# A two-bits-a-round search, pool sums on GpSimd, and the sample's attention placed within the attention units

## What is computed

```python
def layer(x, pos, attn_fn, pool_prev, conv_prev, p):
    h = rms_norm(x, p['g_pre_mix'])
    q, k, v, qi, ki, wi, xp = project(h, p['w_in'], pos)       # q, k, qi, ki rotated (rope)
    a = attn_fn(q, k, v, qi, ki, wi)
    m = pool_mixer(concat([pool_prev, xp], axis=1), T, p['w_pool'], p['pool_scale'])
    mix = concatenate([a, m], axis=-1) @ p['w_out']
    ...                                                        # residual, then the conv FFN

def indexer_scores(qi, wi, ki, q_pos, k_pos):
    dots = einsum('bqhd,bld->bqhl', qi, ki) * (IDX_DIM ** -0.5)
    s = einsum('bqhl,bqh->bql', relu(dots), wi) * (N_IDX_HEADS ** -0.5)
    return where(k_pos <= q_pos, s, -inf)

# prompt: for each block of 128 queries, the 128 best keys; sample: the 256 best of 2049
_, sel = lax.top_k(sc, topk)
p = softmax(where(sel <= q_pos, (q . k[sel]) * HEAD_DIM ** -0.5, -inf)); o = p . v[sel]

def pool_mixer(x_ext, n_out, w_pool, pool_scale):              # windows 2, 4, 8, 16
    diff = wsum / count - xg[:, R - n_out:]
    return einsum('btgc,gcd->btgd', diff, w_pool) * pool_scale
```

## Time and profile before

| | us |
|---|---|
| three runs | 1645.15, 1647.72, 1647.85 (median 1647.72) |
| the profiled execution | 1663.7 |
| span of its trace (first to last instruction) | 1661.9 |
| PE busy, PEld busy | 1499.6 (90%), 1288.6 (78%) |
| DVE busy, ACT busy, POOL busy | 810.7 (49%), 433.2 (26%), 144.3 (9%) |
| mean granted TensorE clock | 0.893 |

### The profile page before, as it was taken

How to read it: one execution, slowest core, us unless ns; L and a number is a source line. 1 busy time by engine, 2 the same in 40 slices (tenths; PEclk the granted TensorE clock), 3 DMA queues, 4 the chain that set the end, 5 groups by cost and what they waited for, 6 DMA issues and landing times. The chain is left out here.

```text
span 1661.9 us, 25466 instructions
## 1 busy us (share of the span) xinstructions
PE 1499.6 (90%) x9736; PEld 1288.6 (78%) x9736; DVE 810.7 (49%) x1716; ACT 433.2 (26%) x753; POOL 144.3 (9%) x160
## 2 busy tenths in 40 slices
PE   4999867899799999999998987699988999999995
PEld 3765744579699999999957556445878999999995
DVE  1137776242665555722142587742346565655221
ACT  3112023333422222522131120233333222224220
POOL 1000301200300000000040022040011000000002
PEclk8999965579899999999979999556789999999997
DMA  8870110102122222222259301010021222222221
GB/s 327 158 112 1 32 60 16 37 1 77 51 94 96 88 88 89 95 79 97 93 209 141 75 25 42 26 51 1 26 77 64 88 88 95 94 76 105 77 102 52
DMA packets 46317, 133.18 MB, mean 80 GB/s; under 512 B 6319, under 2 KB 25615, under 8 KB 38911
## 3 DMA queue, kind: packets, MB, share of 16 engines
q1 hardware_dynamic: 43423, 119.52, 24.9%
q0 software_dynamic: 2816, 12.62, 2.2%
HBM read 119.93 MB, written 12.82 MB: 80 GB/s over the span
## 5 line engine op out<-in xcount | busy, mean ns | idle before, releaser
L746 PE MATMUL ps<-moR_r,W_r 128*128 128x260 f32 x1408 | 286.1, 285 | 0.0
L746 PEld LDWEIGHTS ps<-moR_r,W_r 128*128 128x128 f32 x1408 | 219.1, 190 | 0.0
L746 PE MATMUL ps<-hT_r,QZC_r 128*128 128x260 f32 x896 | 185.1, 289 | 0.0
L746 PE MATMUL ps<-moR_r,QZC_r 128*128 128x260 f32 x704 | 146.7, 290 | 13.1 <-DVE hT_r L1756 12.8
L746 PEld LDWEIGHTS ps<-hT_r,QZC_r 128*128 128x128 f32 x896 | 143.0, 195 | 0.0
L746 PE MATMUL ps<-moR_r,SQ_r 128*128 128x260 f32 x704 | 142.1, 283 | 0.0
L746 PE MATMUL ps<-hT_r,SQ_r 128*128 128x260 f32 x704 | 140.5, 281 | 0.0
L733 PE MATMUL ps<-hT,W 128*128 128x260 f32 x576 | 139.0, 395 | 0.5 <-issue 0.5
L746 PEld LDWEIGHTS ps<-moR_r,QZC_r 128*128 128x128 f32 x704 | 110.8, 192 | 16.7 <-issue 8.5
L733 PEld LDWEIGHTS ps<-hT,W 128*128 128x128 f32 x576 | 109.9, 195 | 17.4 <-issue 1.1
L746 PEld LDWEIGHTS ps<-moR_r,SQ_r 128*128 128x128 f32 x704 | 108.6, 189 | 0.1
(11 more groups left out here) (304 smaller groups left out, 2791.0 us busy)
## 6 DMA issues: line engine op xcount, KB each, us to landing
W<-in_w_gates SPq DMA_DIRECT2D x44, 512.0 KB, 3.3
W<-in_w_vals SPq DMA_DIRECT2D x44, 512.0 KB, 3.3
W<-in_w_downs SPq DMA_DIRECT2D x16, 1408.0 KB, 6.0
W<-in_w_pairs SPq DMA_DIRECT2D x12, 1024.0 KB, 7.8
pages_by_slot<-moR SPq DMA_DIRECT2D x8, 1024.0 KB, 5.1
yR<-pages_by_slot SPq DMA_DIRECT2D x16, 512.0 KB, 19.5
W<-in_w_outs SPq DMA_DIRECT2D x8, 1024.0 KB, 4.8
W<-in_w_kv SPq DMA_DIRECT2D x2, 1312.0 KB, 10.5
```

The lines of the kernel that those rows point to most:

```text
L746: last = mm(ps[:, 2 * (g % 2) + f, 0:HT], w(k), x(k)[:, f * HT:(f + 1) * HT], start=(k == 0 and n == 0), stop=(k == nk - 1 and n == 2))
```

## The change

What is computed stays the same function of the inputs. What changes is this.

- The search tries **three candidates a round** and fixes two bits (`bit_pair`): 17 counts in place of 32. A round has three count operations of 128 x 129 in place of one, and two small operations in place of one ahead of the next candidates. PE sums three columns at a time.
- Rounds still run from d = 11 on. Beside the dots, a round is followed by one rank step in place of two; beside the query tiles by two in place of one. Pending counts are popped after **every fourth k** of a query tile in place of every second, and **pick_a, pick_b, pick_c** are popped there too; after the last round DVE does four rank steps and the last rotation. Units 0 to 3 have no rank steps now; 4 to 15 share the rest.
- The ends of the window sums go from DVE to **POOL** (`pooled`: five operations a window, after the last `cos_part` and before the list's DMA).
- The **pool tiles** go to unit 14 of PE's and ACT's order, as four matmuls of 512 columns and four of 8. SP's `load(9)` waits for these.
- The heads of a block are taken in the order 0, 4, 1, 5, ..., and the scores of the first block wait for the rotations of their own tile (PE has still waited for the last partner to be read).
- The sample's work moves: pick_d's operations to DVE units 0 to 3, its list to PE unit 6, pick_e from unit 14 to 9, keys turned at 21 to 24, scores at 26 and 28, softmax at 30 to 32, and the turn and the values of the sample to PE units 33 and 34, ahead of the last unit's values. ACT's `upper_out(0)` and DVE's `lower_mixed(0..3)` and `lower_out(0)` go from behind the units into them.
- Several tiles change their place in SBUF so that these lifetimes don't overlap.

The diff, cut to its core (ts, tt, stt are tensor_scalar, tensor_tensor and scalar_tensor_tensor on DVE):

```diff
-BITS = 31
+COUNTS = 2 + PAIRS
 SCORED = 10
-ROPES = {21: (4,), 25: (5,), 29: (6,), 31: (7,)}
-POOLED = {26: (0,), 27: (1,), 28: (2,), 30: (3,)}
-DVE_STEPS = 231
+ROPES = {16: (4,), 18: (5,), 19: (6,)}
+HEADS = (0, 4, 1, 5, 2, 6, 3, 7)
+DVE_STEPS = 211
 SPLITS = 2 * NF + 2 * KD
 
...
-                wait_alone(sp, *tile_done(l, WO_T))
+                wait_alone(sp, *pms_mm(l, 1))
                 load(9)
...
+            def pooled(l, g):
+
+                w = WINDOWS[g]
+                res = (LA[:, 0], LB[:, 0], LA[:, 2], LB[:, 2])[g]
+                edge = const("edge")[:, POOL_BUF * g:POOL_BUF * (g + 1)]
+                nc.gpsimd.tensor_tensor(res[:, 15:30], res[:, 15:30], edge, ALU.mult).then_inc(edge_done.sem, 1)
+                wait_alone(gp, *edge_done(l, 3 * g + 1))
+                nc.gpsimd.tensor_scalar(res[:, 15:527], res[:, 15:527], 1.0 / w, None, ALU.mult
+                                        ).then_inc(edge_done.sem, 1)
+                nc.gpsimd.tensor_scalar(DIFF[:, g, SEQ:TOK], XS[:, g, :], 1.0 / w - 1.0, None, ALU.mult
+                                        ).then_inc(edge_done.sem, 1)
+                wait_alone(gp, *edge_done(l, 3 * g + 3))
+                nc.gpsimd.tensor_tensor(DIFF[:, g, 0:SEQ], res[:, 15:527], XPb[:, g, 15:527], ALU.subtract
+                                        ).then_inc(diff_ready.sem, 1)
+                nc.gpsimd.tensor_tensor(DIFF[:, g, SEQ:TOK], DIFF[:, g, SEQ:TOK], prevs_all[:, l, 8 * g:8 * g + 8],
+                                        ALU.add).then_inc(diff_ready.sem, 1)
...
-                    if extras and k % 2:
+                    if extras and k % 4 == 3:
                         extras.pop(0)()
...
                             pe.wait_ge(*dot_relu(l, 24))
-                        mm(ps[:, count_bank(s), 300:301], const("same"), (cntB if s % 2 else cntA),
+                        n = 1 if s < 2 else 3
+                        mm(ps[:, count_bank(s), 300:300 + n], const("same"), tallies[s % 2][:, 0:n],
                            start=True, stop=True).then_inc(cnt_mm.sem, 1)
...
-                counts = [count(s) for s in range(1 + BITS)]
+                counts = [count(s) for s in range(COUNTS)] + [pick_a, pick_b, pick_c]
...
-                for step in counts:
-                    step()
-
                 pe.wait_ge(*rot_used(l, 8))
-                arrived(l, 7)
-                wp = wslot(7)[:, 0:512].rearrange("p (g d) -> p g d", g=4)
-                for g in range(4):
-                    pe.wait_ge(*evac(l, PM_T + g - 1))
-                    pe.wait_ge(*diff_ready(l, 2 * g + 2))
...
+                def pool_tiles():
+                    arrived(l, 7)
+                    wait_alone(pe, *list_ev(l, 1))
+                    pe.wait_ge(*o_ev(l, 1))
+                    wp = wslot(7)[:, 0:512].rearrange("p (g d) -> p g d", g=4)
+                    for g in range(4):
+                        pe.wait_ge(*evac(l, PM_T + g - 1))
+                        pe.wait_ge(*diff_ready(l, 2 * g + 2))
+                        mm(ps[:, 3 + 3 * (g % 2), :], wp[:, g, :], DIFF[:, g, 0:SEQ],
+                           start=True, stop=True).then_inc(tile_done.sem, 1)
+                    pe.wait_ge(*evac(l, PM_T + 3))
+                    for g in range(4):
+                        last = mm(ps[:, 3, NB * g:NB * (g + 1)], wp[:, g, :], DIFF[:, g, SEQ:TOK], start=True, stop=True)
+                    last.then_inc(pms_mm.sem, 1)
...
-                picks = {1: pick_a, 3: pick_b, 5: pick_c, 9: pick_d, 30: sample_scores, 32: scores_by_row}
-                picks.update({25 + q: (lambda q=q: keys_turned(q)) for q in range(4)})
+                picks = {6: pick_d, 14: pool_tiles, 26: sample_scores, 28: scores_by_row, 33: sample_probs_turned,
+                         34: sample_values}
+                picks.update({21 + q: (lambda q=q: keys_turned(q)) for q in range(4)})
 
                 def scores(i):
-                    t, h = divmod(i, N_HEADS)
+                    t, h = i // N_HEADS, HEADS[i % N_HEADS]
                     rows = slice(64 * (h // 4), 64 * (h // 4) + 64)
+                    if t == 0:
+                        pe.wait_ge(*rope_done(l, 5 + h % 4))
                     if i == 0:
-                        pe.wait_ge(*rope_done(l, 8))
-                        pe.wait_ge(*evac(l, WO_T))
+                        pe.wait_ge(*evac(l, PM_T))
...
                 def count(s):
-                    src, by = (S, 0.0) if s == 0 else (S2, cand)
-                    ts(J[:, :], src[:, :], by, None, ALU.is_ge, ALU.add, accum_out=(cntB if s % 2 else cntA)
-                       ).then_inc(cnt_ready.sem, 1)
+                    src, n = (S, 1) if s == 0 else (S2, 1 if s == 1 else 3)
+                    for i in range(n):
+                        last = ts(unread[i], src[:, :], cand(s, i).bitcast(F32) if s else 0.0, None, ALU.is_ge, ALU.add,
+                                  accum_out=tallies[s % 2][:, i:i + 1])
...
+                def bit_pair(s):
+
+                    n = 1 if s == 1 else 3
+                    b = 2 * (PAIRS + 1 - s)
                     dve.wait_ge(*cnt_mm(l, s + 1))
-                    then_wait(ts(candI[:, 1:2], counted(s), kth, float(1 << b), ALU.is_lt, ALU.mult))
-                    if b:
...
+                        then_wait(ts(passed_by, counted(s), kth, None, ALU.is_lt, ALU.add, accum_out=fails))
+                        then_wait(ts(fell, fails, float(1 << b), None, ALU.mult))
+                    top = cand(s, n - 1)
+                    if s + 1 < COUNTS:
+                        then_wait(stt(cands[(s + 1) % 2], bits[:, 3 * s - 3:3 * s], fell, top.broadcast_to([P, 3]),
                                       ALU.bitwise_or, ALU.bitwise_xor))
                         count(s + 1)
...
+                steps = [bits_start, bits_sign] + [lambda s=s: bit_pair(s) for s in range(1, COUNTS)] + [pick_b, pick_c]
...
-                        rank(2 if d >= 16 else 0)
+                        rank(1 if d >= 16 else 0)
                     else:
-                        rank(1)
+                        rank(2)
                     for j in ROPES.get(n, ()):
                         rope(j)
-                    for g in POOLED.get(n, ()):
-                        pooled(g)
-
-
-                def pick_a():
+                rank(4)
+                rope(7)
...
-                picks = {0: pick_a, 2: pick_b, 4: pick_c, 6: pick_d, 14: pick_e}
+                picks = {0: slots, 1: hot_high, 2: hot_low, 3: hot_rows, 9: pick_e, 30: sample_max, 32: sample_probs}
...
-                    if i < 2 * N_HEADS:
+                    if 4 <= i < 2 * N_HEADS:
                         rank(-(-len(ranks) // (2 * N_HEADS - i)))
...
+                    if i in (18, 20, 22, 24):
+                        lower_mixed(range(i // 2 - 9, i // 2 - 8))
+                    elif i == 28:
+                        lower_out(0)
```

More of the change, by code:

```diff
@@ L118, in constants @@
     c.view(np.int32)[:, lo:hi] = 0
-    for b in range(31):
-        c.view(np.int32)[:, lo + b] = 1 << b
+    for r in range(PAIRS):
+        for i in range(3):
+            c.view(np.int32)[:, lo + 3 * r + i] = (i + 1) << 2 * (PAIRS - 1 - r)
+    c.view(np.int32)[:, lo + 3 * PAIRS] = 1 << 2 * PAIRS
     return c
@@ L308, in build @@
         snew = sb("snew", [8, 1])
-        cols = sb("cols", [P, 16])
+        cols = sb("cols", [P, 20])
         sgn, kth, cntA, cntB, offs, need = (cols[:, i:i + 1] for i in range(6))
+        fails, passed_by = cols[:, 9:10], cols[:, 16:19]
+        tallies = [cols[:, a:a + 3] for a in (10, 13)]
+        unread = [yR[:, 3072 + 129 * i:3201 + 129 * i] for i in range(3)]
         snegc = cols[0:64, 6:7]
-        candI = sb("candI", [P, 2], I32)
+        candI = sb("candI", [P, 8], I32)
         IDX = sb("IDX", [P, NB, 2], I32)
@@ L852, in go, with pick_a, pick_b, pick_c @@
                             pe.wait_ge(*dot_relu(l, 24))
-                        mm(ps[:, count_bank(s), 300:301], const("same"), (cntB if s % 2 else cntA),
+                        n = 1 if s < 2 else 3
+                        mm(ps[:, count_bank(s), 300:300 + n], const("same"), tallies[s % 2][:, 0:n],
                            start=True, stop=True).then_inc(cnt_mm.sem, 1)
                     return go
-                counts = [count(s) for s in range(1 + BITS)]
+                def pick_a():
+                    wait_alone(pe, *pick_ready(l, 2))
+                    mm(ps[:, 4, 304:305], const("same"), cntA, start=True, stop=True).then_inc(pick_mm.sem, 1)
+                    mm(ps[:, 4, 305:306], const("below"), cntB, start=True, stop=True).then_inc(pick_mm.sem, 1)
+                def pick_b():
+                    wait_alone(pe, *pick_ready(l, 3))
+                    mm(ps[:, 4, 306:307], const("below"), cntA, start=True, stop=True).then_inc(pick_mm.sem, 1)
+                    mm(ps[0:64, 4, 307:308], const("newto"), J[:, 128:129], start=True, stop=True
```

(7 more changed lines are left out.)

289 lines of the change are left out of this document (150 added, 139 removed).

## The result

The changed kernel took **1588.49 us** (median of 4 runs, 1585.85 to 1601.40) against 1647.78 before (4 runs): ratio 0.966, interval 0.961 to 0.971. The profiled execution took 1585.85 us (span 1584.1, mean granted clock 0.932, before 0.893); the page has PE busy 1435.0 us, where it was 1499.6, though PE does nearly the same work.

What follows compares the result with a forecast made beforehand. The prediction took DVE and PE as nearly full beside the dots, PE to bound the query tiles, round trips the first scores, DVE units 0 to 15; terms summed to −12.6 us a layer, giving 1623 us, range 1603 to 1647.

Steps and rivals of the forecast that it cites:

- A, the dots: Search rounds beside the dots: longer rounds with three counts on DVE, +3.6 us a layer (bounds +2.3 and +5.0).
- B and C: Query tiles, PE-bound with fewer pops, −4.9 us a layer; then to first scores, a shorter chain of round trips, −13.1.
- D, units 0 to 15: DVE-bound units: more rank steps, the pool tiles and POOL holds outweigh removed picks, +6.4 us a layer.
- The hold by POOL: Units 0 to 3: POOL's moved sums hold DVE operations for 2.5 us a layer, a quarter of 10.4.
- E: Unit 16 to the output projection: fewer waits at the end and behind the gather, −4.6 us a layer (bounds −8, +5).
- rival 3: Fast stretch at 328.4 to 341.0 us loses its clock, costing 12.6 a layer: about 1647 us, chance 0.13.
- the waits that go: Before the output projection: sample's softmax and values chain moves beside units 30 to 32, −3.0 us a layer.
- the loss behind "remote": Middle units: DVE stood still 8.57 us during the gathers, PE lost 4.21; half taken as gone, −2.1 a layer.
- 1 (slower by the gather): Units 11 to 17: the earlier gather holds DVE while it is the bound; about 1654 us, chance 0.10.
- 2 (time comes back in the units): Units 0 to 15: full DVE–POOL holds (+7.9 a layer) or costlier rank steps and pool tiles; about 1638 us, chance 0.17.
- 4: Whole layer: all unknowns fall well, with no POOL hold and the gather stall gone; −21.5 a layer, 1605 us, chance 0.10.
- signs named for "wrong": PE waiting at query-tile counts, one-hot operations above 3 us, DVE idle in units 11 to 17, clock fallen before output projection.

Runs made afterwards that it cites:

- a_twice: The changed kernel with each of a round's three counts made twice, the second result unread: 1622.02 us, one execution.
- b_dense16: The kernel before with four added matmuls of 512 columns at PE's unit 16, whose result nobody reads: 1623.46 us, ratio to before 0.987.
- b_again: The kernel before, unchanged, in another profiled execution: 1647.56 us.
- a_pool20: The changed kernel with the pool tiles as one block at unit 20 in place of 14, banks, copies and low parts moved to fit: 1610.13 us.
- a_spread: The changed kernel with the pool tiles one matmul a unit at units 12 to 15 in place of all in unit 14: 1595.80 us.

## Why the prediction was right and wrong

**A, the dots**: forecast +3.6, measured +2.7 (175.7 against 173.0). Right in kind: in a_twice a round grows by what its counts grow, so DVE bounds the rounds.

**B and C**: forecast −4.9 and −13.1. The tiles take 32.6 where they took 38.4 (−5.8), and from the last tile to the first scores 6.3 where it was 19.3 (−13.0). Right. Taking cover and chain apart by stage was enough here; none of the PE waits at pops that I named as a danger is longer than 0.49 us in the tiles. No experiment undid the search alone; these two rest on the stage lengths of the two traces.

**D, units 0 to 15**: forecast +6.4, measured +9.4 against the earlier trace rows's execution between first scores and unit 16, +8.6 between the masks of units 0 and 16. The hold by POOL was forecast at 2.5 and measured at 2.6, but that it met is luck: a quarter was a guess, made since most operations there have one input from SBUF, and 1.74 of the 2.6 fell on just such operations. The pool tiles were forecast at 3 and measured at 4.0; the rank steps were eleven more, not ten. The rule that the prediction took from the Trainium skill (SBUF — State Buffer, Who interferes with whom) fits the one-hot operation, which has two inputs from SBUF. For the scalings, which have one, the same section of the Trainium skill lets a `tensor_scalar` contend when it runs in a two-port mode; that they did, no row here shows. The page Perfetto Trace Analysis of the Trainium skill, that moving work to GpSimd might not help, did not decide anything: the price is these 2.6 us, and what DVE was spared is part of C.

**E is the step that failed**: −4.6 forecast, −28.2 measured from unit 16 to the output projection. Another 1.2 us came behind it: the output projection starts at 0.50 in both, and is back at 1.00 after 3.2 us in place of 6.0, so that its first 40 records end 1.2 us sooner. The sum priced units 16 to 31 at the durations of the earlier trace rows and of their trace, at half clock, and asked only which waits would go. It said nothing of why the clock was 0.58 in one stretch and 1.00 in another, and rival 3 knew the clock only as something to lose, at a place (328 to 341 us) chosen since it was fast. I had the pool tiles' matmuls at unit 14 as a cost on PE, 3 to 6.8 us; that they raise the clock for what follows is the whole surprise. In numbers, with the second execution of before as the measure: −11.6 in units 16 to 23, by the clock; −12.2 from unit 24, of which b_dense16 with the old order of the tail gets 6.4 (52.6 to 46.2) by the clock, so that 5.8 are left for the moved softmax and values. (In layer 2 these are −9.4, 3.6 and again 5.8.) The forecast of 3.0 for the waits that go was right there, and most of the rest is the values' own time, 7.00 before and 3.74 now, which is the clock once more.

**A second fault lay in the base.** Half of the loss behind "remote", −2.1 a layer, was booked as a gain; another execution does not have the loss. The 16 us between profile and median were in view and were only passed on to the sum; they should have made every single stall in that trace suspect. The hold explains about half of the 16: units 16 to 23 were 4.3 a layer longer with it. Against b_again the stages sum to −28.6 in layer 1 and −25.3 in layer 2, −54 of the −59 between the medians; the output projections give another 2, and the rest was not followed.

**The rivals.** 1 (slower by the gather): no DVE wait behind "remote" in any trace of the changed kernel. 2 (time comes back in the units): partly, 3.0 of the 7.9 that it named. 3 (a fast stretch lost): not seen. The clock falls behind the sample's scores for 12.7 us, but it did so before too (335.4 to 345.6 us in b_again), and the units ahead gained a fast stretch. 4 named −21.5 a layer as the best case; the measured −29 lies beyond even the lower ends of A to E together (−26.7), since no term let PE's own durations change. Two of the signs named for "wrong" came, a one-hot operation of above 3 us (3.15) and a granted clock that has fallen ahead of the output projection; neither is what failed.

## What to carry to other kernels

Read the granted clock of each stretch beside its busy time before pricing anything in it: a stretch at 0.50 with PE busy throughout is not bound by its work but by a clock that something ahead of it did not raise. A reorder that puts long matmuls right ahead of many short ones can be worth more than all the waits that it removes: b_dense16 gained 21 us by nothing else. Whether taking out short waits between matmuls does the same was not tried by itself. And take the base from an execution that is near the median; a stall seen once is checked in a second trace before it is booked.

## What the runs showed of the hardware

- PE busy without a gap does not by itself raise the clock: 29.3 us of the kernel before (b_again) and 16 us in a_pool20 passed at 0.50, with matmuls of 128 and 384 columns. The same units ran at 1.00 behind the pool tiles (17.7 us). So the same code ran through at either level.
- It rose within four matmuls of 512 columns (after, a_pool20, b_dense16), and with such matmuls between units (a_spread); it fell behind 16 matmuls of 8 columns (in 20 layers of 20; in two of six when they were split in three), behind two waits of 0.7 us (a_spread), and beside the dots when each round's wait grew (a_twice).
- Such a block is one way, not the only one. In b_again the clock rose at 263.7 us behind 128 bf16 matmuls of 32 columns, with no wait of PE beside them, and fell at 270.5 with two short waits; it rose again at 321.7, in unit 26, with nothing added. The scores of 256 columns show the rise (1.22, then 0.70), the turned probabilities the fall (0.44, then 0.69 for the same two records):

```profile
259.13 1.22 PE L972 MATMUL ps<-kT,QQ 64*128 64x256 f32 x2
260.28 3.57 PE L930 MATMUL ps<-yR 128*16 128x32 bf16 x128
...
264.40 0.70 PE L972 MATMUL ps<-kT,QQ 64*128 64x256 f32 x2
...
268.61 0.44 PE L981 MATMUL ps<-C,moR 128*128 128x128 f32 x2 [0.58 <-DVE moR L1686]
...
271.02 0.69 PE L981 MATMUL ps<-C,moR 128*128 128x128 f32 x2 [0.77 <-DVE moR L1686]
```

- What in a stretch of matmuls raises the clock stays open: these runs show that a block of long ones did, not why it did where busy short ones did not.
- DVE and POOL hold each other: an operation of 2.29 us became 3.15 on DVE and one of 0.29 became 0.98, and one of 0.24 became 2.14 on POOL.
- Why the profiled execution of before had DVE stopped for 8.57 us in both layers, and b_again with the same program not, stays open.
